# Attention scores of two 64-column heads side by side in the array, their additive rows loaded through DRAM and added by VectorE

## The reference, cut to what matters

```python
def forgetting_attention(q, k, v, cum_logf):          # layer 0 of the second block
    s = einsum(q, k) * scale
    s = s + cum_logf[..., qs:qe, None] - cum_logf[..., None, :qe]
    p = softmax(where(causal, s, -inf));  out = p @ v

def chunk_band_attention(q, k, v, rel_table):         # layer 1 of the second block
    bias = rel_table[:, clip(row - column, -128, 128) + 128]
    s = einsum(q, k) * scale + bias
    p = softmax(where(valid, s, -inf));  out = p @ v
```

## Time and profile before

| | us |
|---|---|
| median of three runs (1920.12 to 1921.67) | 1920.56 |
| the profiled execution | 1921.43 |
| its span in the trace | 1919.6 |
| PE busy | 1896.6 |
| DVE busy | 1297.8 |
| ACT busy | 1126.7 |
| POOL busy | 329.4 |

### The profile page before, as it was taken

The page is one execution under the profiler, slowest core; times in us unless marked ns, Lnnn a source line. Parts: engine busy times, 40 slices in busy tenths (PEclk is TensorE's granted clock), DMA queues, the critical chain, the costliest instruction groups (busy, mean ns, idle before and its releaser), DMA issues.

```text
span 1919.6 us, 25057 instructions
## 1 busy us (share of the span) xinstructions
PE 1896.6 (99%) x9153; PEld 1640.8 (85%) x9153; DVE 1297.8 (68%) x1915; ACT 1126.7 (59%) x1689; POOL 329.4 (17%) x555
## 2 busy tenths in 40 slices
PE   9999999999999999999999999999999999999999
PEld 7888888888888888888887888888888888788888
DVE  6687676566877775666577765766666566856664
ACT  6586555455866654655467665654555465665552
POOL 1110232101100531022100000431122111101220
PEclk9999999999999999999999999999999999999999
DMA  8865688778657997698754354997788676646884
GB/s 278 255 204 189 194 262 251 241 219 250 203 188 216 282 281 228 190 261 257 237 160 154 121 186 147 281 275 239 224 252 258 224 246 201 212 147 190 250 257 141
DMA packets 282602, 424.80 MB, mean 221 GB/s; under 512 B 24908, under 2 KB 161312, under 8 KB 282480
## 3 DMA queue, kind: packets, MB, share of 16 engines
q1 hardware_dynamic: 256144, 352.41, 59.2%
q0 software_dynamic: 25872, 70.45, 13.6%
q10 hardware_dynamic: 464, 0.34, 0.1%
HBM read 389.54 MB, written 33.57 MB: 220 GB/s over the span
## 4 chain that ended last, share of the span: by engine, by line
PE 91%; DVE 4%; ACT 3%; issue 1%; DMA 1%; ACTq 0%; POOL 0%; DVEq 0%
PE M L946 28%; PE M L948 28%; PE M L947 28%; DVE WL L1494 1%; PE AUX L990 1%; ACT WH L1233 1%; PE AUX L1202 1%; PE AUX L1180 1%; ACT TMP L1268 0%; DVE SM L1680 0%; PE AUX L1004 0%; PE AUX L1126 0%; DMA RAW<-in_x_w_q 0%; DVE TMP L1637 0%; PE AUX L1141 0%
## 5 line engine op out<-in xcount | busy, mean ns | idle before, releaser
L1494 DVE TENSOR_TENSOR WL<-RAW,WH 128x1024 fp32r<-128x1024 f32 (+1 forms) x670 | 810.9, 1215 | 461.6 <-ACT WH L1233 459.1
L1233 ACT ACTIVATE WH<-RAW 128x1024 fp32r<-128x1024 f32 (+1 forms) x670 | 704.1, 1054 | 524.5 <-PE M L948 500.8
L946 PE MATMUL M<-WH,Bh 128*128 128x512 f32 x1792 | 690.3, 385 | 1.5 <-DVE Bl L1521 0.7
L948 PE MATMUL M<-WH,Bl 128*128 128x512 f32 x1792 | 680.3, 380 | 0.0
L947 PE MATMUL M<-WL,Bh 128*128 128x512 f32 x1792 | 680.2, 380 | 0.0
L946 PEld LDWEIGHTS M<-WH,Bh 128*128 128x128 f32 x1792 | 339.4, 189 | 51.0 <-issue 3.8
L948 PEld LDWEIGHTS M<-WH,Bl 128*128 128x128 f32 x1792 | 339.3, 189 | 48.4
L947 PEld LDWEIGHTS M<-WL,Bh 128*128 128x128 f32 x1792 | 339.6, 190 | 45.5
L1263 ACT ACTIVATE AS<-M,KEEP 128x256 f32<-128x256 f32 x132 | 55.2, 469 | 81.5 <-PE M L948 81.5
L946 PE MATMUL M<-WH,MTh 128*128 128x512 f32 x128 | 53.8, 421 | 0.0
L947 PE MATMUL M<-WL,MTh 128*128 128x512 f32 x128 | 48.5, 379 | 0.0
(11 more groups left out here) (457 smaller groups left out, 2794.3 us busy)
## 6 DMA issues: line engine op xcount, KB each, us to landing
RAW<-in_ffn_w_in SPq DMA_DIRECT2D x352, 256.0 KB, 3.8
RAW<-in_w_in SPq DMA_DIRECT2D x103, 512.0 KB, 4.8
RAW<-in_w_gate_up SPq DMA_DIRECT2D x176, 256.0 KB, 4.3
RAW<-in_ffn_w_out SPq DMA_DIRECT2D x88, 512.0 KB, 4.6
RAW<-in_w_down SPq DMA_DIRECT2D x44, 512.0 KB, 4.7
RAW<-in_x_w_kv SPq DMA_DIRECT2D x32, 512.0 KB, 3.7
RAW<-in_even_w_in SPq DMA_DIRECT2D x24, 512.0 KB, 4.4
RAW<-in_odd_w_in SPq DMA_DIRECT2D x24, 512.0 KB, 4.7
```

Of the source, the lines that this page charges most:

```text
L946: e.matmul(out, s.hi, wh, start=s.at0, stop=False)
L948: i = e.matmul(out, s.lo, wh, start=False, stop=s.final)
L1233: e.activation(p.WH[:, h, 0:s.size], p.RAW[:, i, 0:s.size], ACT.Copy).then_inc(k.w_hi, 1)
L1494: e.tensor_tensor(p.WL[:, h, 0:s.size], p.RAW[:, s.u % NRAW, 0:s.size], hi.bitcast(F32), ALU.subtract).then_inc(k.w_lo, 1)
```

## The change

Scores: Q now lies like K, two heads over 128 partitions, without zeros. The scores of the two heads of a pair are issued together, each head's in its own half of the array's rows, by the lines that the differential attention uses already (1097 to 1109). The two products per part that added the forget row and the bias are gone from PE.

Additions: a new tile `NB` (128 x 8 x 384) holds the negated forget rows of all heads, spread over all partitions. POOL writes `NCT` (8 x 256) to DRAM, waits for it and reads it back twice with a partition step of zero (`nctld`). DVE adds the causal mask to it once (`nctma`), and the additions per head read `NB` instead of the mask. For the bias, `H` grows to 128 x 8 x 384 in row order; DVE adds the chunk mask once (`hmask`) and adds `H` to all 384 score columns per head.

The table: to read `H` in row order, DRAM holds 128 copies of the table (1.57 MB). POOL writes them from partitions 0 to 7 with four DMAs of 32 copies in `su_tab`. `hload` reads 1.5 MB in three DMAs.

Order: the heads are laid out by pairs, with the steps of the second head 1.2 or 1.3 positions behind the first, the division at +4.2, the transposes at +5.6 and +6.8, the values at +8.2. Layer 0 starts 0.6 positions sooner, layer 1 starts 1.7 later. The clearing of Q and its copies in two halves are gone.

```diff
-    def heads(self, at, gap, lag, lab_o, names, V, Q, K, vals, extra, diag, A):
+    def heads(self, at, gap, lab_o, names, V, Q, K, vals, extra, A):
         for hp in range(4):
-            pts = []
+            b = at + 2 * gap * hp
+            ss, pts = [], []
             for hh in range(2):
-                h = 2 * hp + hh
-                b = at + gap * h
                 s = self.add("hg_s", b)
-                s.h, s.q, s.k = h, Q[:, h, :], K[:, hp, :]
+                s.late = 1.3 * hh
+                s.h, s.mate = 2 * hp + hh, ss[0] if hh else None
+                s.q, s.k = (x[64 * hh:64 * hh + 64, hp, :] for x in (Q, K))
...
-                f = self.add("hg_p", b + 3.2 + lag / 2)
...
+                f = self.add("hg_p", b + 4.2 + 1.2 * hh)
...
-                t = self.add("pt", b + 4.2 + lag)
+                t = self.add("pt", b + 5.6 + 1.2 * hh)
-            o = self.add("hg_o", b + 5.4 + lag)
+            o = self.add("hg_o", b + 8.2)
...
+        ld = self.add("nctld", c.end + 8.5)
...
+        ma = self.add("nctma", c.end + 24.0)
...
-        self.heads(c.end + 1.0, 2.75, 0.8, lab_o, ["aq0", "aq1", "ak0", "ak1"], VA, QA, KA, av, "forget", False, A)
+        self.heads(c.end + 0.4, 2.75, lab_o, ["aq0", "aq1", "ak0", "ak1"], VA, QA, KA, av, S["NB"], A)
...
-        e0 = c.end + 24.0
+        e0 = c.end + 25.7
...
-        self.heads(e0, 3.0, 1.0, lab_o, ["dq0", "dq1", "dk0", "dk1"], VD, QD, KD_, dv, "bias", True, A)
+        self.add("hmask", e0 - 6.0)
+        self.heads(e0, 3.0, lab_o, ["dq0", "dq1", "dk0", "dk1"], VD, QD, KD_, dv, self.H, A)
...
+            elif s.extra is p.H:
+                e.tensor_tensor(aux[:, 0:384], aux[:, 0:384], s.extra[:, s.h, :], ALU.add).then_inc(k.dve_chain, 1)
...
+        elif s.kind in ("nctma", "hmask"):
+            x, mask = (s.NB, p.CAUSAL[:, P:2 * P]) if s.kind == "nctma" else (p.H, p.CHUNK)
...
+            for i in (0, 2):
+                v = x[:, :, i * P:(i + 1) * P]
+                e.tensor_tensor(v, v, mask.unsqueeze(1).to_broadcast([P, 8, P]), ALU.add).then_inc(k.dve_chain, 1)
...
         elif s.kind == "su_tab":
             e.wait_ge(k.su_tab, 1)
-            e.dma_start(p.scratch, p.TB[0:8, 0:384]).then_inc(k.d_tabx, 16)
+            for i in range(4):
+                e.dma_start(p.scratch[32 * i:32 * i + 32].rearrange("p h c -> h p c"),
+                            p.TB[0:8, 0:384].unsqueeze(1).to_broadcast([8, 32, 384])).then_inc(k.d_tabx, 16)
...
+            for i, off in enumerate((255, 127, 255)):
+                e.dma_start(p.H[:, :, i * P:(i + 1) * P],
+                            bass.AP(p.scratch.tensor, p.scratch.offset + off, [[8 * 384 - 1, P], [384, 8], [1, P]])).then_inc(k.d_h, 16)
+        elif s.kind == "nctld":
+            e.wait_ge(k.aux_out[s.ct.bank], s.ct.use)
+            e.dma_start(p.parked_nct, s.rows[0:8, :]).then_inc(k.d_nct, 16)
+            e.wait_ge(k.d_nct, 16)
+            x = p.parked_nct
+            e.dma_start(s.NB[:, :, 0:P], bass.AP(x.tensor, x.offset, [[0, P], [256, 8], [1, P]])).then_inc(k.d_nb, 16)
+            e.dma_start(s.NB[:, :, P:3 * P], bass.AP(x.tensor, x.offset, [[0, P], [256, 8], [1, 256]])).then_inc(k.d_nb, 16)
```

More of the change, by code:

```diff
@@ L732, in even_mixer @@
         c = self.chunk("aq", B, 0, KD, lab)
-        self.head_qk(c, nm, 8, "aq", ("heads", lambda t: QA[:, :, t * P:(t + 1) * P], self.gq["a"], None))
-        for t in range(T):
-            self.turned[f"aq{t}"].zero = z
+        self.head_qk(c, nm, 8, "aq", ("plain", cols(QA), self.gq["a"], None))
         c = self.chunk("ak", B, 0, KD, lab)
@@ L753, in odd_mixer @@
         room = S["room"]
-        self.head_qk(c, nm, 8, "dq", ("heads", lambda t: QD[:, :, t * P:(t + 1) * P], self.gq["d"], None), room)
-        for t in range(T):
-            self.turned[f"dq{t}"].zero = z
+        self.head_qk(c, nm, 8, "dq", ("plain", cols(QD), self.gq["d"], None), room)
         c = self.chunk("dk", B, 0, KD, lab)
         self.head_qk(c, nm, 8, "dk", ("plain", cols(KD_), self.gk["d"], None), room)
-        e0 = c.end + 24.0
+        e0 = c.end + 25.7
         c = self.chunk("cc", B, 0, KD, lab)
@@ L1096, in tensor @@
             e.matmul(aux[:, 264:272], tri[:, 0:128], s.lf[:, 8:16], start=False, stop=True).then_inc(k.aux_full[b], 1)
-        elif s.kind == "df_s":
+        elif s.kind in ("df_s", "hg_s"):
             for x in s.turned:
@@ L1109, in tensor @@
                 e.matmul(aux[:, 128:384], s.q[:, P:256], s.k[:, 0:256], start=True, stop=True).then_inc(k.aux_full[b], 1)
[L1110 to L1134, removed]
         elif s.kind == "pt":
@@ L1741, in vector @@
             e.wait_ge(k.aux_full[b], s.use)
-            if s.kind == "df_s" or s.diag:
+            if s.kind == "df_s":
                 if s.n == 1:
@@ L1798, in vector @@
             if s.n == 1:
-                e.wait_ge(k.zeroed, 2)
+                e.wait_ge(k.zeroed, 1)
                 for x in s.turned:
@@ L1875, in vector @@
             e.wait_ge(k.d_tab, 16)
-            e.tensor_copy(p.TB[0:8, 257:384], p.TB[0:8, 256:257].to_broadcast([8, 127])).then_inc(k.su_tab, 1)
+            e.tensor_copy(p.TB[0:8, 0:127], p.TB[0:8, 127:128].to_broadcast([8, 127])).then_inc(k.su_tab, 1)
+        elif s.kind in ("nctma", "hmask"):
+            x, mask = (s.NB, p.CAUSAL[:, P:2 * P]) if s.kind == "nctma" else (p.H, p.CHUNK)
+            e.wait_ge(*((k.d_nb, 32) if s.kind == "nctma" else (k.d_h, 48)))
+            e.wait_ge(k.d_c2, 16)
+            for i in (0, 2):
+                v = x[:, :, i * P:(i + 1) * P]
+                e.tensor_tensor(v, v, mask.unsqueeze(1).to_broadcast([P, 8, P]), ALU.add).then_inc(k.dve_chain, 1)
+                chain += 1
+            e.wait_ge(k.dve_chain, chain)
 def gpsimd(e, k):
@@ L2004, in sync, with build_program @@
     e.wait_ge(k.d_out, 16 * 2 * len(p.outs))
-def build_program(nc, a, out, scratch, squares):
+def build_program(nc, a, out, scratch, squares, parked_nct):
     with ExitStack() as ctx:
         p = Plan(a)
-        p.out, p.scratch, p.parked, p.outs = out, scratch, squares, []
+        p.out, p.scratch, p.parked, p.parked_nct, p.outs = out, scratch, squares, parked_nct, []
         sb = lambda name, shape, dt=F32, c=ctx, **kw: c.enter_context(nc.sbuf_tensor(name, shape, dt, **kw))
@@ L2179 @@
     out = nc.dram_tensor("out_x", (1, T * P, D), F32, kind="ExternalOutput").ap()
-    scratch = nc.dram_tensor("table", (8, 384), F32, kind="Internal").ap()
+    scratch = nc.dram_tensor("table", (P, 8, 384), F32, kind="Internal").ap()
     squares = nc.dram_tensor("squares", (PARKED, 4 * P * 256), F32, kind="Internal").ap()
-    build_program(nc, aps, out, scratch, squares)
+    parked_nct = nc.dram_tensor("forget_rows", (8, 256), F32, kind="Internal").ap()
+    build_program(nc, aps, out, scratch, squares, parked_nct)
     r = _run(nc, [arrays], core_ids=[0])
```

59 lines of the change are left out of this document (29 added, 30 removed).

## The result

The changed kernel takes 1930.7 us, median of four runs (1929.6 to 1935.7), against 1921.1 us for the kernel before: 1.0055 of it, 95% interval 1.004 to 1.007. It is slower by 9.6 us. One later run, of the kernel with the table in 32 partitions, took 2818.8 us at a granted clock of 0.66 and is left out of its median. The profiled execution has a span of 1928.3 us where the kernel before has 1919.6, so 8.7 us are to be found in the traces.

What follows compares the result with a forecast made beforehand. PE was taken to set the time nearly everywhere (99% busy), DVE in three short places. 1921.4 - 8.1 (heads together) + 12.9 (table write) = 1926.2 profiled, median 0.9 lower, said as 1925; range 1908 to 1932.

Steps and rivals of the forecast that it cites:

- The slow write: Favoured case, chance 0.60: the table write in layer 0 is slow, L 22 to 38 us, kernel at 1917 to 1933.
- the sign that the forecast gave itself: Forecast is wrong if L is below 20 us, or PE's chunks near 310 don't depend on the feed-forward exchange.
- Scores: Score products of the heads: a pair costs PE 1.05 us, so PE loses 12.6 us of work, 6.3 per layer.
- Layer 0: Heads -2.7 us, clock loss included; ACT's copies and the mask in the differential attention -2.05; together -4.75.
- the forecast's list of 13.9 us: Layer 0, last pair: DVE's work up to the division takes 13.9 us, PE needs 11.1, so PE stands 2.8.
- Layer 1: Heads of layer 1: -6.3 of work, -2.0 old waits, +5.0 new waits, -3.3 us; 1.7 less if the clock falls.
- Masks and loads: Mask before the differential attention's first division delays PE 0.35 us; `NB` lands about 1016, before 1017.9; `hmask` and `hload` cost nothing.
- Table write: Feed-forward exchange queued behind the four DMAs comes late: PE stands 10.2 us, clock 1.7, weights about 1: +12.9 us.
- L: Time from the table write's first issue until all four DMAs are through: taken as 30 us, between 14 and 93.
- ACT needs it at 305.36: ACT needs the exchange at 305.36, in order; PE stands from L = 19.8 us on, each further us costing one.
- The quick write: Rival, chance 0.33: table goes out at its bytes' pace, L up to 20 us; only heads count, 1912.5 (1907 to 1917).
- Full gain: Rival, chance 0.05: pairs leave PE no new waits and the table is quick, 1902.6 us.

## Why the prediction was right and wrong

The slow write, the forecast's case, is what happened, and the time (1930.7 against 1925) lies near the upper end of the range. Two terms were off, on opposite sides: the write by +8.0 us and layer 1 by -4.1. That they half cancel is luck, and so is part of how well the time was met. By the sign that the forecast gave itself, whether PE's chunks near 310 depend on that exchange, its step at the write failed.

**Scores.** From the main product ahead of the pair to the second behind it, 1636.62 - 1635.14 = 1.48 us; less two main products it is 1.05, as forecast. PE's timeline of after:

```profile
1635.14 0.38 PE L950 MATMUL M<-WH,MTl 128*128 128x512 f32 x1
1635.45 0.37 PE L1108 MATMUL AUX<-KD,QD 64*128 64x128 f32 x1
1635.45 0.37 PE L1109 MATMUL AUX<-KD,QD 64*128 64x128 f32 x1
...
1636.30 0.48 PE L948 MATMUL M<-WH,MTh 128*128 128x512 f32 x1
1636.62 0.38 PE L949 MATMUL M<-WL,MTh 128*128 128x512 f32 x1
```

With a head at 1.31 us in layer 0 and 1.32 in layer 1 that is 6.3 and 6.4 us, forecast 6.3. Right.

**Layer 0.** Forecast -4.75, measured -4.6. The mask lies at 1038.5, and the transpose behind it comes 0.27 us late (forecast 0.35). The stand there shrank from 1.98 to 1.05 us (forecast 1.3), and the fall of the clock behind it is gone, as said. The division at the last pair is the forecast's list of 13.9 us, and the stand it gave as 2.8:

```profile
1115.45 0.55 PE L1118 MATMUL AUX<-CC,TMP 128*128 128x128 f32 x3 [2.87 <-DVE TMP L1768]
```

The window behind it has the clock at 0.83, so 1.7 us more, also as said:

```profile
1110.00:1120.00 10.00, 7.13 (x28) 5.62 (x28) 8.19 (x21) 4.28 (x11) 0.77 (x1) 0.83 0.48 148
```

The earlier stand is 0.67 (forecast 0.8). This stretch of the program doesn't settle whether the clock falls there: it did in six of nine profiles that had this stand.

**Layer 1.** Forecast -3.3 without a fall of the clock, measured -7.4, also without one: this term was 4 too small. The new stands came to 0.3 + 0.7 + 2.5 = 3.5 us (over an undisturbed transpose), forecast 5.0. The 1.0 at 1605 that "stays" is gone with the pairs' new places in ACT's order. The other 2.1 us lie behind the heads, at a place that the forecast never looked at. PE's waits of the kernel before have a line for it:

```profile
PE AUX L990 <- DVE X L1558: 1.7, 1, 1.7
```

In after PE doesn't stand there. That is no gain of the change. In every other kernel with the change, PE stands there for 0.95 to 2.7 us; in before and in the kernel with the divisions sooner, ACT waits 3.6 and 3.7 us just ahead of it for weights (`in_x_w_q`). Why ACT waits less for them in after (1.6 us twice) is open. The eight other profiles with the same heads give back 3.2 to 5.5 us in layer 1, seven of them with a fall of the clock of about 1.7 us there or just behind; the one without it, the timed kernel with 32 partitions, gives back 5.5. So some 2 us of the 4 are the forecast's stands, sized too large, and 2 are this profile's.

**Masks and loads.** `NB` is issued at 1018.7 and through at 1031.6; less the 20.6 us of delay that is 1011.0 (forecast 1016, needed 1017.9), and `H` and `hmask` cost nothing: from 1550 to 1622, while they run, PE works 71.87 of 72 us. Right.

**Table write.** L was taken as 30 and is 35.0, and PE was to stand L - 19.8 with 2.7 us of extras: 12.9 forecast, 20.9 measured. With L = 35 the same reckoning gives 17.9. The size of L accounts for 5 us, and the mechanism for 3. The step that failed is "ACT needs it at 305.36": the exchange was not what ACT waited for. The exchange came as late as reckoned, at 328.9 (294.6 + 35.0 = 329.6), but the weights were later still. The forecast counted about 1 us for the weights that share the engines and saw nothing else in that sharing. But weights came at 0.07 MB in 10 us, PE stood from 309.2, 17 us after the first issue, but for one unit until 330.3, 3 us after the write was through. The runs with all, half and a quarter of the copies show it, and so does the write in the kernel before.

**The rivals.** The quick write is what the cures make of it: forecast 1912.5 for that case, and medians of 1910.6 (from DRAM) and 1911.1 (32 partitions) measured. In the profile with the copies from DRAM layer 0 gives back 6.2 us, without a fall of the clock, and layer 1 3.8 with one; 0.7 are won in the first 75 us. Full gain (1902.6) was reached by none; the moved divisions come nearest with a median of 1907.2.

## What to carry to other kernels

Before a transfer goes into a stretch that lives on streamed weights, look at how many partitions it reads and how long its packets hold an engine: a slow packet holds the engine against every other queue. What it costs goes by how long the streamed weights are shut out and how far ahead they were, and not only by the wait of whoever needs the data: writes of 35.0, 20.2 and 10.5 us cost 20.9, 8.1 and 0 us here, with weights converted 7.8 us ahead. The size of a packet alone didn't decide: those of 4608 bytes took 1.31 us from eight partitions and 0.20 from 128. Copying the source to 32 partitions, or letting DRAM be the source, made a cost of 21 us vanish. When a stand is taken away, look further down the timeline (here some 20 us) for the next one before counting it as gained.

## What was not expected of the hardware

- Eight partitions of SBUF gave 54 GB/s over all engines, 32 partitions 194. A packet of 4608 bytes held its engine for 1.31 us against 0.29 us from 32 partitions, and the other queue fell from 204 to 7 GB/s.
- Products in the two halves of the array ran at the same time in whichever order they were written; one started ahead of a product written before it.
- The same stand of PE, 2.9 us at the same instruction, was followed by a fall of the granted clock to the lower level in six of nine profiles. Two profiles of one program (the table in 32 partitions) differ by 1.7 us of span, 1911.0 and 1909.3: one has a fall in layer 1, the other has none there.
